# Seven experts' rows added to a DRAM buffer by an accumulating indirect DMA in place of the combine matmuls

## Chip, core and metric

The kernel runs on one core of a Trainium2 chip. The metric is the device time of one execution in microseconds (us), as a median of several runs.

## The reference

A decoder trunk of two layers for 256 tokens (SEQ) of width 1024 (D). Each layer mixes tokens by three branches (a state space model, dilated attention, attention into a memory), then applies a channel mixer: a dense SwiGLU in layer 0, and in layer 1 a mixture of eight experts of which each token uses two. Only the end of layer 1 is touched by the change:

```
logits = (t @ w_router)                       # t: 256 x 1024, 8 experts
top_v, top_i = lax.top_k(logits, 2)
wts = jax.nn.softmax(top_v, axis=-1)
gate = jnp.sum(jax.nn.one_hot(top_i, 8) * wts[..., None], axis=1)
for e in range(8):
    ye = swiglu(t, w_gate[e], w_up[e], w_down[e])   # 1024 -> 3584 -> 1024
    out = out + gate[:, e:e + 1] * ye
x = x + out
```

All of it is float32. An expert's weights are 44 MB, so that the eight experts read 352 MB from DRAM.

## The kernel before

The token rows lie in SBUF as x, 128 partitions by C = 2 chunks of 1024. All matmuls are done in three passes on a high and a low part of each operand (fp32r), so that float32 accuracy is kept. For the expert stage each weight matrix streams through a ring of RM = 7 tiles of 128 x 2048 floats (1 MB each; six in ring_e, the seventh in hT). An expert has 42 of them (MOE_TILES), 28 of gate and up weights and 14 of down weights. For each tile SyncE issues the load (L516) when VectorE has finished with the tile seven places ahead, ScalarE writes the high part into hi (L1788), VectorE the low part into lo (L2486), and TensorE does 12 matmuls of 512 columns with them (split_product, L736 to L738). hi and lo have three buffers each (H = 3), so that ScalarE starts on tile m when TensorE is done with tile m-3. SyncE, ScalarE, VectorE and TensorE each have their own program in a fixed order and are kept together by semaphores.

An expert works on the up to 128 tokens that chose it. DVE builds a 0/1 matrix `disp` (dispatch), 256 tokens by 128 slots, for two experts at a time; the matmuls of `gather` multiply it with the normed rows (h_hi, h_lo) and give `xe`, the transposed rows of the expert's slots, which are split into xe_hi and xe_lo. The order of the work on TensorE around the end of an expert is written out by hand:

- the last down tiles of expert e finish `y`, 128 slots by 1024, in PSUM banks 4 and 5
- gate_first(e + 1): the first two tiles of the next expert
- the *combine*: eight matmuls of 512 columns (L1344 and L1345) with dispT as the fixed operand and y_hi and y_lo as the moving one, which bring the rows of the slots back to the rows of the tokens in PSUM banks 3, 6, 7 and 2
- then expert(e + 1): its up tiles (2 and 3), two transposes of disp_plain (L1310), which VectorE copies to dispT (L2701), and the steps over the hidden columns.

ScalarE writes y_hi between the high parts of tiles 1 and 2 of the next expert (L1982), VectorE writes y_lo between the low parts (L2734). VectorE's add_rows (L2685) multiplies the four combined pieces with the token's gate and adds them to x, between tiles 3 and 4 of the next expert. After the last expert the adds go by halves and SyncE stores x into the output (L547). If more than 128 tokens chose one expert, a second pass follows; with these inputs none does.

GpSimd builds constants at the start and does small root calculations in the two mixers. In the expert stage it has no work. route_weights on VectorE (L2625 to L2631) computes the gates before the first expert.

Of the kernel before, what the change touches and what calls it, by code (L numbers as in the profile page):

```python
# [20 lines left out]
P = 128  # L21
# [11 lines left out]
def decoder_trunk(nc, x_in, mem_in, positions, norm_mix, w_in, a_re, a_im, log_dt, b_re, b_im,  # L33
# [57 lines left out]
    with ctx:  # L91
# [134 lines left out]
        fb("idle", [P, KD - 3, P])  # L226
        xe_hi = fb("xe_hi", [P, KD, P], F32R)
        xe_lo = fb("xe_lo", [P, KD, P], F32R)
        y_hi = fb("y_hi", [P, D], F32R)
# [15 lines left out]
        TURNS = MOE_TILES // RM  # L245

# [199 lines left out]
        def _(sp):  # L446
# [113 lines left out]
        def _(pool):  # L560
# [109 lines left out]
            for l in range(L):  # L670
# [36 lines left out]
                if l == 0:  # L707
# [4 lines left out]
                    rotary_gains(1)  # L712


        @block.tensor
        def _(pe):
# [490 lines left out]
            def experts():  # L1207
# [90 lines left out]
                def expert(pair, odd, last_one):  # L1298
# [9 lines left out]
                    pe.wait_ge(sem("added"), 4 * e + 1)  # L1308
                    for c in range(C):
                        last = nc.tensor.transpose(ps[:, 3, c * P:(c + 1) * P], disp_plain[:, c, odd, :], ident[:])  # L1310
                    last.then_inc(sem("dispatchT_done"), 1)
# [23 lines left out]
                    pe.wait_ge(sem("dispatchT_ready"), e + 1)  # L1335
                    for c, half in ADD_BY_HALVES if last_one else ADD_BY_ROWS:
                        if (c, half) == (0, 0) and last_one:
                            pe.wait_ge(sem("y_half_ready"), e // NE + 1)
                        elif c == 0 and half == (1 if last_one else 0):
                            pe.wait_ge(sem("y_ready"), e + 1)  # L1340
# [24 lines left out]
                def one_pass(pair0):  # L1365
# [6 lines left out]
                    if pair0 == 0:  # L1372
                        for p in range(NE // 2 - 1):
                            expert(p, 0, False)
                            expert(p, 1, False)
# [4 lines left out]
                    expert(NE // 2 - 1 + pair0, 0, False)  # L1380
# [5 lines left out]
                with pe.If(busiest > P):  # L1386
                    pe.wait_ge(sem("added"), 4 * NE + 1)
# [9 lines left out]
        def _(act):  # L1397
# [484 lines left out]
            def experts():  # L1882
# [53 lines left out]
                def expert(pair, odd, last_one):  # L1936
# [38 lines left out]
                    act.wait_ge(sem("added"), 4 * e + 1)  # L1975
                    rest = slice(0, D)
                    if last_one:
                        rest = slice(BANK, D)
                        act.wait_ge(sem("y_half_done"), e // NE + 1)
                        nc.scalar.activation(y_hi[:, 0:BANK], ps[:, 4, :], ACT.Copy).then_inc(sem("y_half_hi_ready"), 1)  # L1980
                    act.wait_ge(sem("split_used"), M + s0 + MOE_TILES)
                    nc.scalar.activation(y_hi[:, rest], flat_banks(4, 2)[:, rest], ACT.Copy).then_inc(  # L1982
                        sem("y_hi_ready"), 1)
# [3 lines left out]
                def one_pass(pair0):  # L1987
# [10 lines left out]
                    for p in range(NE // 2 - 1):  # L1998
                        expert(p + pair0, 0, False)
# [815 lines left out]
```

## Time and profile before

| | us |
|---|---|
| median of 3 runs | 1757.39 |
| lowest, highest | 1756.54, 1758.14 |
| the profiled execution, its time | 1759.97 |
| the profiled execution, span of the core | 1758.2 |
| mean granted clock of TensorE | 0.995 |

The profile is of one execution. Its times are us from the start of the span. PE is TensorE and PEld its weight loads, DVE is VectorE, ACT is ScalarE, POOL is GpSimd, SP is SyncE; a q behind a name is the engine's sequencer or DMA queue. L12 is line 12 of the kernel. In a row of the timeline stand the start, the duration, engine, line, operation, what is written `<-` what is read, the number of such instructions merged, and in brackets the idle time of the engine before it and what ended it. Matmuls are pipelined: the duration of one is longer than the time until the next starts. In a row of the waits stand who waited, for whom, us in total, how often, and the longest. The mixers and the dense layer take until about 765 us, the expert stage the rest.

### The profile page before, as it was taken

The numbers are of one execution on the slowest core, as the hardware profiler recorded it, in microseconds if no ns is written. First come the engines' busy times: TensorE is split into PE (matmuls) and PEld (weight loads), VectorE is DVE, ScalarE is ACT, GpSimd is POOL, SyncE is SP. The second block draws the span as 40 slices with busy tenths as digits, with TensorE's granted clock in tenths as the row PEclk, the third lists the DMA queues.
The fourth block names the chain that finished last, engine by engine and source line by source line (L and its number), as shares of the span: only waits on it lengthen the run. The fifth ranks groups of instructions, "written<-read, shape, count | busy, mean of one in ns | idle before, by whom it ended". The sixth has DMA issues, their size and how long they took to land.

```text
span 1758.2 us, 23343 instructions
## 1 busy us (share of the span) xinstructions
PE 1738.1 (99%) x8758; PEld 1439.0 (82%) x8758; DVE 1437.6 (82%) x1348; ACT 1191.4 (68%) x1405; POOL 119.6 (7%) x165
## 2 busy tenths in 40 slices
PE   9999999999999999999999999999999999999998
PEld 7778888888888888888888888888888888888886
DVE  8997557776649955768898898898998988988987
ACT  7877564744457756567777777767777767777775
POOL 5160000150002200000000000000000000000000
PEclk9999999999999999989999999999999999999999
DMA  7454336655444443479999999999999999999994
GB/s 242 141 167 142 123 122 214 209 185 180 167 162 152 154 151 120 159 265 369 377 351 338 381 362 367 375 343 360 364 354 374 357 350 379 349 373 374 364 370 166
DMA packets 221226, 477.09 MB, mean 271 GB/s; under 512 B 9357, under 2 KB 34057, under 8 KB 221129
## 3 DMA queue, kind: packets, MB, share of 16 engines
q1 hardware_dynamic: 220328, 474.07, 75.3%
q0 software_dynamic: 704, 1.70, 0.5%
q8 instruction: 62, 1.02, 0.2%
q14 instruction: 36, 0.29, 0.1%
q10 hardware_dynamic: 96, 0.02, 0.0%
HBM read 474.71 MB, written 1.05 MB: 271 GB/s over the span
## 4 chain that ended last, share of the span: by engine, by line
PE 88%; DVE 9%; issue 1%; ACT 1%; DMA 0%; SPq 0%; DVEq 0%; ACTq 0%
PE ps L736 27%; PE ps L738 26%; PE ps L737 26%; DVE ring_lo L2048 3%; PE ps L1271 1%; PE ps L1013 1%; PE ps L729 1%; DVE turned L2306 1%; PE ps L985 1%; DVE z L2264 1%; PE ps L1249 1%; PE ps L996 1%; ACT hi_m L1430 0%; DVE lo L2486 0%; PE ps L1345 0%
## 5 line engine op out<-in xcount | busy, mean ns | idle before, releaser
L2486 DVE TENSOR_TENSOR lo<-ring_e,hi 128x2048 fp32r<-128x2048 f32 x288 | 657.6, 2290 | 78.8 <-ACT hi L1788 76.9
L1788 ACT ACTIVATE hi<-ring_e 128x2048 fp32r<-128x2048 f32 x288 | 551.9, 1917 | 164.5 <-PE ps L738 164.5
L736 PE MATMUL ps<-hi,xe_hi 128*128 128x512 f32 x896 | 354.5, 396 | 1.7 <-DVE lo L2486 0.9
L738 PE MATMUL ps<-hi,xe_lo 128*128 128x512 f32 x896 | 349.6, 390 | 0.0
L737 PE MATMUL ps<-lo,xe_hi 128*128 128x512 f32 x896 | 349.0, 390 | 0.0
L1430 ACT ACTIVATE hi_m<-ring 128x1024 fp32r<-128x1024 f32 x160 | 160.6, 1054 | 115.9 <-PE ps L738 112.5
L2048 DVE TENSOR_TENSOR ring_lo<-ring,hi_m 128x1024 fp32r<-128x1024 f32 x160 | 190.2, 1231 | 33.6 <-ACT hi_m L1430 33.1
L738 PE MATMUL ps<-hi_m,xT_lo 128*128 128x512 f32 (+1 forms) x528 | 203.2, 385 | 0.0
L736 PEld LDWEIGHTS ps<-hi,xe_hi 128*128 128x128 f32 x896 | 168.3, 188 | 38.1 <-issue 3.7
L738 PEld LDWEIGHTS ps<-hi,xe_lo 128*128 128x128 f32 x896 | 168.2, 188 | 36.0
L737 PEld LDWEIGHTS ps<-lo,xe_hi 128*128 128x128 f32 x896 | 168.4, 188 | 33.2
L736 PE MATMUL ps<-hi,aT_hi 128*128 128x512 f32 x464 | 181.6, 391 | 0.1
L738 PE MATMUL ps<-hi,aT_lo 128*128 128x512 f32 x464 | 180.8, 390 | 0.0
L737 PE MATMUL ps<-lo,aT_hi 128*128 128x512 f32 x464 | 180.5, 389 | 0.0
L736 PE MATMUL ps<-hi_m,in_hi 128*128 128x512 f32 (+1 forms) x416 | 165.0, 397 | 5.1 <-DVE ring_lo L2048 3.8
L737 PE MATMUL ps<-ring_lo,in_hi 128*128 128x512 f32 (+1 forms) x416 | 159.6, 384 | 0.0
L2486 DVE TENSOR_TENSOR lo<-hT,hi 128x2048 fp32r<-128x2048 f32 x48 | 109.9, 2289 | 14.4 <-ACT hi L1788 14.1
L738 PEld LDWEIGHTS ps<-hi_m,xT_lo 128*128 128x128 f32 x528 | 99.7, 189 | 20.3
L1788 ACT ACTIVATE hi<-hT 128x2048 fp32r<-128x2048 f32 x48 | 92.0, 1916 | 20.8 <-PE ps L738 20.8
L736 PEld LDWEIGHTS ps<-hi,aT_hi 128*128 128x128 f32 x464 | 87.1, 188 | 18.3 <-issue 0.5
L738 PEld LDWEIGHTS ps<-hi,aT_lo 128*128 128x128 f32 x464 | 87.1, 188 | 18.3
L737 PEld LDWEIGHTS ps<-lo,aT_hi 128*128 128x128 f32 x464 | 87.2, 188 | 17.9
(422 smaller groups left out, 2464.5 us busy)
## 6 DMA issues: line engine op xcount, KB each, us to landing
ring_e<-in_moe_w_gate SPq DMA_DIRECT2D x104, 1024.0 KB, 6.9
ring_e<-in_moe_w_up SPq DMA_DIRECT2D x96, 1024.0 KB, 7.0
ring_e<-in_moe_w_down SPq DMA_DIRECT2D x88, 1024.0 KB, 6.7
ring<-in_w_in SPq DMA_DIRECT2D x50, 1024.0 KB, 5.0
hT<-in_moe_w_down SPq DMA_DIRECT2D x24, 1024.0 KB, 6.1
hT<-in_moe_w_up SPq DMA_DIRECT2D x16, 1024.0 KB, 6.4
ring<-in_ffn_w_gate SPq DMA_DIRECT2D x22, 512.0 KB, 3.9
ring<-in_ffn_w_up SPq DMA_DIRECT2D x22, 512.0 KB, 4.8
```

Of the source, the lines that this page charges most:

```text
L729: last = nc.tensor.transpose(o, a, ident[0:a.shape[0], 0:a.shape[0]])
L736: nc.tensor.matmul(o, x_hi, w_hi, start=first, stop=False, skip_group_check=True)
L737: nc.tensor.matmul(o, x_hi, w_lo, start=False, stop=False, skip_group_check=True)
L738: return nc.tensor.matmul(o, x_lo, w_hi, start=False, stop=end, skip_group_check=True)
L985: last = nc.tensor.matmul(ps[:, bank, col:col + nk], qkT[o:o + HD, 0, hd // 2, c * P:(c + 1) * P], qkT[o:o + HD, 1, hd // 2, 0:nk], start= ...
L996: nc.tensor.transpose(ps[:, 6 + b // 4, b % 4 * P:(b % 4 + 1) * P], pr[:, u % 2, b * P:(b + 1) * P], ident[:])
L1013: last = nc.tensor.matmul(ps[:, 5, o:o + v.shape[1]], pT[:, b * P:(b + 1) * P], v, start=first, stop=end, skip_group_check=True)
L1249: last = nc.tensor.matmul(o, part_[:, c, k * P:(k + 1) * P], disp[:, c].rearrange("p i s -> p (i s)"), start=i == 0 and c == 0, stop=i == ...
L1430: nc.scalar.activation(hi_m[:, m % 2, o], ring[:, n % R, o], ACT.Copy).then_inc(sem("mixer_hi_ready"), 1)
L1788: nc.scalar.activation(hi[:, m % H, :], src, ACT.Copy).then_inc(sem("hi_ready"), 1)
L2048: V.tensor_tensor(ring_lo[:, n % R, o], ring[:, n % R, o], hi_m[:, m % 2, o].bitcast(F32), ALU.subtract).then_inc(sem("mixer_lo_ready"), 1)
L2486: last = V.tensor_tensor(lo[:, m % H, :], src, hi[:, m % H, :].bitcast(F32), ALU.subtract)
```

## The change

Experts 0 to 6 are no longer combined by matmuls. A DRAM buffer `sums` of 384 rows is set to x (256 rows, and 128 spare rows). When an expert's `y` is finished, ScalarE writes it to SBUF as y_rows, multiplied with the gate of each slot's token, and GpSimd issues one indirect DMA that adds each of the 128 rows to the row of `sums` of its token; empty slots add to a spare row. At the end of the seven, GpSimd loads `sums` back into x, and the last expert (7) is combined and added as before.

Where the slot's token, whether it is filled, and its gate come from: a matrix `routes` (256 tokens by 8 experts by 4 values: the token's number, a one, and the high and low part of the gate) is multiplied with `disp` in two matmuls of 4 columns for each expert, in place of the two transposes of disp_plain. VectorE copies the result (128 x 4) to slot_values, and GpSimd computes with five small operations the row number and the gate of each slot.

The new small tiles take their room from the unused tile `idle`; each takes a multiple of 32 bytes, 480 in all, as `idle` loses, so that xe_hi, the gathered operand, stays at a multiple of 1024 bytes. y_rows lies at the place of y_hi. The second pass, if any, works as before.

```diff
-        fb("idle", [P, KD - 3, P])
+        routes = fb("routes", [P, C, NE, 4], F32R)
+        token_i = fb("token_i", [P, C], I32)
...
+        slot_gate = fb("slot_gate", [P, 1])
+        fb("idle", [P, (KD - 3) * P - 120])
...
+        y_rows = renamed("y_rows", [P, D], F32)
...
+        sums = nc.dram_tensor("sums", [SEQ + P, D], F32).ap()
@@ sync
-                sp.wait_ge(sem("added"), 4 * (NE - 1) + 3 + 2 * half)
+                sp.wait_ge(sem("added"), 3 + 2 * half)
@@ gpsimd
+            def expert_rows():
+                pool.wait_ge(sem("h_ready"), C)
+                pool.wait_ge(sem("h_hi_ready"), C)
+                chain(nc.gpsimd.iota(token_i[:], pattern=[[P, C]], base=0, channel_multiplier=1))
+                chain(nc.gpsimd.tensor_copy(token[:], token_i[:]))
+                nc.gpsimd.tensor_scalar(spare_row[:], token[:, 0:1], float(SEQ), None, ALU.add)
+                nc.gpsimd.tensor_copy(routes[:, :, :, 0], spread(token[:], 2, NE))
+                nc.gpsimd.tensor_copy(routes[:, :, :, 1], ones[:, 0:C * NE].rearrange("p (c e) -> p c e", c=C)).then_inc(
+                    sem("route_rows_ready"), 1)
+                pool.dma_start(sums[0:SEQ].rearrange("(c p) d -> p c d", p=P), x[:]).then_inc(sem("sums_set"), 16)
+                pool.dma_start(sums[SEQ:SEQ + P], x[:, 0, :]).then_inc(sem("sums_set"), 16)
+                for e in range(NE - 1):
+                    pool.wait_ge(sem("slot_values_taken"), e + 1)
+                    chain(nc.gpsimd.tensor_scalar(row_of[:], slot_values[:, 1:2], -1.0, 1.0, ALU.mult, ALU.add))
+                    chain(nc.gpsimd.tensor_tensor(row_of[:], row_of[:], spare_row[:], ALU.mult))
+                    chain(nc.gpsimd.tensor_tensor(row_of[:], row_of[:], slot_values[:, 0:1], ALU.add))
+                    if e > 0:
+                        pool.wait_ge(sem("rows_added"), 16 * e)
+                    chain(nc.gpsimd.tensor_copy(row_i[:], row_of[:]))
+                    nc.gpsimd.tensor_tensor(slot_gate[:], slot_values[:, 2:3], slot_values[:, 3:4], ALU.add).then_inc(
+                        sem("slots_ready"), 1)
+                    if e == 0:
+                        pool.wait_ge(sem("sums_set"), 16 * 2)
+                    pool.wait_ge(sem("rows_ready"), e + 1)
+                    pool.indirect_dma_start(sums, bass.IndirectOffsetOnAxis(row_i[:, 0:1], 0), y_rows[:], None,
+                                            compute_op=ALU.add).then_inc(sem("rows_added"), 16)
+                pool.wait_ge(sem("rows_added"), 16 * (NE - 1))
+                pool.dma_start(x[:], sums[0:SEQ].rearrange("(c p) d -> p c d", p=P)).then_inc(sem("x_summed"), 16)
@@ tensor: expert, scattered is True for experts 0 to 6
+                    if scattered:
+                        pe.wait_ge(sem("added"), 1)
+                        pe.wait_ge(sem("routes_ready"), 1)
+                        pe.wait_ge(sem("route_rows_ready"), 1)
+                        if e > 0:
+                            pe.wait_ge(sem("slot_values_taken"), e)
+                        for c in range(C):
+                            last = nc.tensor.matmul(ps[:, 3, 0:4], disp[:, c, odd, :], routes[:, c, e, :], start=c == 0,
+                                                    stop=c == C - 1)
+                        last.then_inc(sem("slot_values_done"), 1)
...
                     if not last_one:
                         gate_first(e + 1)
-                    pe.wait_ge(sem("dispatchT_ready"), e + 1)
+                    if scattered:
+                        pe.wait_ge(sem("rows_ready"), e + 1)
+                        return
@@ scalar: expert
+                    if scattered:
+                        act.wait_ge(sem("slots_ready"), e + 1)
+                        if e > 0:
+                            act.wait_ge(sem("rows_added"), 16 * e)
+                        act.wait_ge(sem("split_used"), M + s0 + MOE_TILES)
+                        nc.scalar.activation(y_rows[:], flat_banks(4, 2), ACT.Copy, scale=slot_gate[:]).then_inc(
+                            sem("rows_ready"), 1)
@@ vector: route_weights
+                chain(V.tensor_copy(routes[:, :, :, 2], gate[:]))
+                V.tensor_tensor(routes[:, :, :, 3], gate[:], routes[:, :, :, 2].bitcast(F32), ALU.subtract).then_inc(
+                    sem("routes_ready"), 1)
@@ vector: expert, no add_rows and no y_lo where scattered
+                    if scattered:
+                        dve.wait_ge(sem("slot_values_done"), e + 1)
+                        if not first_one:
+                            dve.wait_ge(sem("slots_ready"), e)
+                        V.tensor_copy(slot_values[:], ps[:, 3, 0:4]).then_inc(sem("slot_values_taken"), 1)
...
                     if last_one:
+                        if first_pass:
+                            dve.wait_ge(sem("x_summed"), 16)
                         add_rows(e_here, e, ADD_BY_HALVES)
```

## Rows read from the trace of the kernel before

**Rows 1.** The page's busy times: us, share of the span, instructions.
```profile
PE 1738.1 (99%) x8758; PEld 1439.0 (82%) x8758; DVE 1437.6 (82%) x1348; ACT 1191.4 (68%) x1405; POOL 119.6 (7%) x165
```
**Rows 2.** The waits of all engines from 850 to 1740 us.
```profile
ACT hi L1788 <- PE ps L738: 168.5, 197, 2.2
...
PEld ps L736 <- issue: 3.5, 7, 0.5
```
**Rows 3.** The waits of SyncE's own DMA queue in the same stretch.
```profile
SPq L516 <- DVE lo L2486: 698.8, 303, 4.2
```
**Rows 4.** Timeline of TensorE around the combine of expert 2.
```profile
1147.27 0.39 PE L1344 MATMUL ps<-y_hi,dispT 128*128 128x512 f32 x1
...
1149.08 0.39 PE L736 MATMUL ps<-hi,xe_hi 128*128 128x512 f32 x1
...
1154.52 0.38 PE L1310 MATMUL ps<-ident,disp_plain 128*128 128x128 f32 x2
1154.66 0.47 PE L736 MATMUL ps<-hi,xe_hi 128*128 128x512 f32 x1
```
**Rows 5.** Instructions on disp_plain: ns min/median/max, first and last start us.
```profile
L1310 PE MATMUL ps<-ident,disp_plain x16: 270/270/271, 790.5 to 1642.5; 128*128 128x128 f32 x16
```
**Rows 6.** Stretch of seven experts: PE, PEld, DVE, ACT, POOL busy; clock; DMA share; GB/s.
```profile
790.50:1642.50 852.00, 851.25 (x3892) 704.14 (x3891) 770.29 (x467) 622.23 (x413) 0.00 (x0) 1.00 0.99 363
```
**Rows 7.** Timeline of TensorE: small matmuls and the gather matmuls.
```profile
770.47 0.35 PE L1233 MATMUL ps<-sel,before_r 128*128 128x8 f32 x1
770.68 0.35 PE L1234 MATMUL ps<-sel,ones_r 128*128 128x8 f32 x1
...
1160.90 0.40 PE L1249 MATMUL ps<-disp,h_lo 128*128 128x256 f32 x2
1161.14 0.40 PE L1249 MATMUL ps<-disp,h_hi 128*128 128x256 f32 x2
```
**Rows 8.** Timeline of VectorE between experts 2 and 3.
```profile
1143.71 1.22 DVE L2734 TENSOR_TENSOR y_lo<-ps,y_hi 128x1024 fp32r<-128x1024 f32 x1
...
1149.25 2.72 DVE L2685 SCALAR_TENSOR_TENSOR x<-ps,gate,x 128x512 f32<-128x512 f32 x4
```
**Rows 9.** Timeline of ScalarE between the same experts.
```profile
1141.73 1.03 ACT L1982 ACTIVATE y_hi<-ps 128x1024 fp32r<-128x1024 f32 x1 [0.80 <-PE ps L738]
1142.65 1.91 ACT L1788 ACTIVATE hi<-ring_e 128x2048 fp32r<-128x2048 f32 x1
...
1147.96 1.91 ACT L1788 ACTIVATE hi<-ring_e 128x2048 fp32r<-128x2048 f32 x1
```
**Rows 10.** Timeline of VectorE and TensorE before the first expert.
```profile
785.11 0.17 DVE L2631 TENSOR_TENSOR gate<-gate,rstat 128x16 f32<-128x16 f32 x1
785.32 2.29 DVE L2486 TENSOR_TENSOR lo<-ring_e,hi 128x2048 fp32r<-128x2048 f32 x1
...
787.67 0.50 PE L736 MATMUL ps<-hi,xe_hi 128*128 128x512 f32 x1 [0.94 <-DVE lo L2486]
```
**Rows 11.** Timeline of VectorE and GpSimd in the dense layer.
```profile
378.31 0.42 DVE L2168 TENSOR_TENSOR b_tmp_next<-b_raw_next,spT 128x256 f32<-128x256 f32 x1
...
380.00 2.13 DVE L2168 TENSOR_TENSOR b_tmp_next<-b_raw_next,spT 128x256 f32<-128x256 f32 x1
...
379.76 2.08 POOL L625 TENSOR_TENSOR cT<-cT,spT 128x1024 f32<-128x1024 f32 x1 [4.96 <-ACT cT L1854]
```
**Rows 12.** Timeline: issue of expert 3's first tile, and its first reader.
```profile
1120.71 3.09 SPq L516 DMA_DIRECT2D ring_e<-in_moe_w_gate  x2
...
1136.80 1.91 ACT L1788 ACTIVATE hi<-ring_e 128x2048 fp32r<-128x2048 f32 x1
```
**Rows 13.** Loads into ring_e from 850 to 1740 us, issue to landing.
```profile
DMA to landing us min/median/max: 4.8/6.8/8.2
```
**Rows 14.** DMA in 744 to 764 us, GB/s in 40 slices.
```profile
GB/s 0 41 16 303 389 397 406 430 163 234 315 422 393 328 385 406 410 401 418 406 414 393 418 406 418 397 406 418 414 401 402 418 414 406 401 418 397 422 397 418
```
**Rows 15.** The page's DMA issues: KB each, median us from issue to landing.
```profile
out<-x SPq DMA_DIRECT2D x2, 512.0 KB, 3.7
```

More of the change, by code:

```diff
@@ L1296, in gate_first, with expert @@
                     hidden(0, FFN_TILES, MOE_TILES * e, e)
-                def expert(pair, odd, last_one):
+                def expert(pair, odd, last_one, scattered=False):
                     e = 2 * pair + odd
@@ L1306, in expert @@
                     hidden(1, M + 2, s0)
[L1308 to L1311, printed above, removed]
+                    if scattered:
[8 more added lines that the diff above has]
+                        last.then_inc(sem("slot_values_done"), 1)
+                    else:
+                        ci = combines_before(e)
+                        pe.wait_ge(sem("added"), 4 * ci + 1)
+                        pe.wait_ge(sem("slot_values_taken"), NE - 1)
+                        for c in range(C):
+                            last = nc.tensor.transpose(ps[:, 3, c * P:(c + 1) * P], disp_plain[:, c, odd, :], ident[:])
+                        last.then_inc(sem("dispatchT_done"), 1)
                     def step(f, shift, first, between=None, gathers=None):
@@ L1386, in experts @@
                 with pe.If(busiest > P):
-                    pe.wait_ge(sem("added"), 4 * NE + 1)
+                    pe.wait_ge(sem("added"), 4 * combines_before(NE) + 1)
                     one_pass(NE // 2)
@@ L1934, in gathered_high, with expert @@
                         sem("xe_hi_ready"), 1)
-                def expert(pair, odd, last_one):
+                def expert(pair, odd, last_one, scattered=False):
                     e = 2 * pair + odd
@@ L1973, in expert @@
                             split(i, e + 1)
[L1975 to L1983, printed above, removed]
+                    if scattered:
[5 more added lines that the diff above has]
+                            sem("rows_ready"), 1)
+                    else:
+                        act.wait_ge(sem("added"), 4 * combines_before(e) + 1)
+                        act.wait_ge(sem("rows_added"), 16 * (NE - 1))
+                        rest = slice(0, D)
+                        if last_one:
+                            rest = slice(BANK, D)
+                            act.wait_ge(sem("y_half_done"), e // NE + 1)
+                            nc.scalar.activation(y_hi[:, 0:BANK], ps[:, 4, :], ACT.Copy).then_inc(
+                                sem("y_half_hi_ready"), 1)
+                        act.wait_ge(sem("split_used"), M + s0 + MOE_TILES)
+                        nc.scalar.activation(y_hi[:, rest], flat_banks(4, 2)[:, rest], ACT.Copy).then_inc(
+                            sem("y_hi_ready"), 1)
                     if not last_one:
@@ L1998, in one_pass @@
                     for p in range(NE // 2 - 1):
-                        expert(p + pair0, 0, False)
-                        expert(p + pair0, 1, False)
-                    expert(NE // 2 - 1 + pair0, 0, False)
+                        expert(p + pair0, 0, False, not base)
+                        expert(p + pair0, 1, False, not base)
+                    expert(NE // 2 - 1 + pair0, 0, False, not base)
                     expert(NE // 2 - 1 + pair0, 1, True)
@@ L2687, in add_rows, with expert @@
                                                ALU.add).then_inc(sem("added"), 1)
-                def expert(e_here, pair, odd, first_one, last_one):
+                def expert(e_here, pair, odd, first_one, last_one, scattered=False):
                     e = 2 * pair + odd
+                    ci = combines_before(e)
+                    first_pass = scattered or last_one and isinstance(e, int) and e < NE
                     a0 = NF + NFE * e
@@ L2694, in expert @@
                     split(3, e)
-                    if not first_one:
+                    if not first_one and not first_pass:
                         add_rows(e_here - 1, e - 1)
@@ L2725, in expert @@
                             split(i, e + 1)
+                    if scattered:
+                        split(2, e + 1)
+                        return
                     rest = slice(0, D)
```

39 lines of the change are left out of this document (25 added, 14 removed).

## The prediction

> **What bounds the kernel now.** I read the page's busy times first, and only as a question: TensorE is busy for 99% of the span [rows 1], but ends of matmuls are modelled, and the weights stream from DRAM all the while, so it could as well be the DMA. The waits of the expert stage (850 to 1740 us) answer it. ScalarE waits for TensorE to hand back a half buffer, 168.5 us in total; TensorE's only entry is 3.5 us in seven pieces of 0.5 us [rows 2]. The queue of SyncE, which issues the weight loads, sat for 698.8 of 890 us until VectorE had finished with a ring buffer [rows 3]: the loads are not late, they wait for room. So TensorE sets the pace. The timeline says how fast: eight combine matmuls start at 1147.27 and the next weight matmul at 1149.08, so 0.226 us for each 512-column matmul, whatever their 0.39 us of pipelined duration. One expert has 42 tiles of 12 such matmuls, 504 x 0.226 = 114 us; the transposes of disp_plain, two an expert, give its period, (1642.5 - 790.5)/7 = 121.7 us [rows 5]. The other 7 are the combine 1.8, transposes, gathers and a stall of half a us. In those 852.0 us TensorE is busy for 851.3 [rows 6]. There is no slack on TensorE: an instruction taken out there is time.
>
> **What is removed.** For experts 0 to 6, TensorE loses the eight combine matmuls: 8 x 0.226 = 1.81 us each, 7 x 1.81 = **12.7 us**. They lie bare on the path, between two weight matmuls, with no wait before or after [rows 4]. ScalarE's y_hi becomes y_rows, the same size from the same banks in the same place (1.03 us; with a scale from a tile I allow 0.1 more) and gains nothing. VectorE loses y_lo (1.22 us) and four adds into x (2.72 us) [rows 8]. Those are off the path (VectorE is idle a tenth of the stage [rows 6]), so I count them zero; they buy slack.
>
> **What is swapped.** Two transposes of disp_plain (next instruction 0.14 us after the first: 1154.52 to 1154.66 [rows 4]) become two matmuls of four columns with disp as operand. No such matmul is in the trace. Below: as cheap as the transposes, 0.14 the pair. Above: the eight-column matmuls at 770.47, 0.21 each, 0.42 the pair, though right behind a wait of TensorE. Nearest are the gather matmuls, each with one 128x128 weight load as well, 0.12 each (two pairs 0.24 apart) [rows 7]: 0.24. So +0.1 each, 7 x 0.1 = **0.7 us** lost (bounds 0 and 2.0).
>
> **What is added on VectorE at the start.** Two small operations behind L2631 split the gates, at a spacing of 785.11 to 785.32, 0.21 each. Here VectorE *is* the path: they stand in front of the split of tile 3, and TensorE idled 0.94 us at 787.67 for exactly that [rows 10]. **0.4 us** lost (bounds 0 and 0.4).
>
> **GpSimd and the new DMAs.** GpSimd does nothing in the expert stage now [rows 6]. Five small operations an expert, an indirect DMA of 128 rows of 4 KB, and at the ends 1.5 MB stored to sums and 1 MB read back. The store starts when h_lo is done, before the first expert, the read-back right behind the scatter of expert 6, 115 us before the last expert's adds ask for it (wait for x_summed). Each scatter likewise has a whole expert until rows_added is asked for. As latency all is hidden, even at many times the 3.7 us of the 0.5 MB store of the output [rows 15]. If the cover were gone, each us would count once. What can hurt is sharing. An expert's weights are 42 tiles of 1024 KB, 44.04 MB in 121.7 us, 362 GB/s; in the first fill, with the queue full, the later slices show 393 to 422 [rows 14]. After the change the need is 367 plus the scatter: 0.52 MB plainly moved is 1.3 us at 410, with the destination read as well 2.6 us. Tile 0 of the next expert was issued at 1120.71 and first read at 1136.80, 16.1 us later [rows 12]; landing takes 6.8 us, 8.2 at worst [rows 13]. So 7.9 us of slack against 1.3 to 2.6 us of push, and room of 40 GB/s to recover it before the next. Cost zero.
>
> **New waits.** TensorE waits for rows_ready where it waited for dispatchT_ready and y_ready: after gate_first of the next expert. y_rows is done when y_hi was, 1141.73 + 1.03 = 1142.76 [rows 9], and TensorE comes at 1147.27: no stall. But it now runs on to tile 2 at 1147.27 instead of 1149.08. Is tile 2 split? ScalarE's half ends at 1142.65 + 1.91 = 1144.56 [rows 9], VectorE's takes 2.29 more [rows 10], 1146.9: 0.4 us to spare, 0.3 with a longer y_rows. Tile 4: ScalarE ends 1147.96 + 1.91 = 1149.87, VectorE 1152.2; TensorE comes at 1147.27 + 5.44 (24 matmuls, 1149.08 to 1154.52 [rows 4]) + 0.24 = 1152.95: 0.8 to spare. This margin is thin, so I bound it: 0, which I take, to 0.5 us an expert, 3.5 in all, the size of the stalls already there. Those seven (start of tile 0, 0.5 us against a regular 0.23) stay; were they to go, 7 x 0.27 = 1.9 gained. x_summed, routes_ready and route_rows_ready are ready long before they are asked for, if GpSimd's first five operations fit between the second h_lo and 790.5, where L1310 stands now [rows 5]. The new `idle` with the new small tiles is to leave xe_hi where it stood; I count no effect.
>
> **Sum.** 12.7 - 0.7 - 0.4 = 11.6 us gained; bounds 12.7 - 2.0 - 0.4 - 3.5 = 6.8 and 12.7 + 1.9 = 14.6. The profiled execution took 1759.97 us (span 1758.20 and 1.77 around it), 2.6 over the median 1757.39. So 1748.4 for one like it, and a median of 1757.4 - 11.6 = **1745.8 us**, own range 1742.8 to 1750.6.
>
> **Rivals.** (A) *The scatter holds the weight loads; slower.* If an accumulate must read a row, add and write it before its engine takes another packet, 8 rows an engine go one after the other. The 0.5 MB store lands in 3.7 us [rows 15], of which 1.3 are bytes at 410 GB/s, so 2.4 are the way there and back; 8 x 2.4 = 19 us, less 7.9 of slack, 11 us of stall x 7 = 78, time 1757.4 + 78 - 11.6 = 1824. It decides from 7.9 + 11.6/7 = 9.6 us of delay a scatter. For: nothing in the trace shows that it doesn't, none of its DMAs accumulates. Against: each tile lands in 6.8 us while a new one is asked for every 2.9 (121.7/42), so the engines hold packets of two or three transfers at once already.
>
> (B) *DMA is the true pace.* If 362 GB/s is what the chip gives this stream, removing matmuls only exposes loads, and each scatter adds 1.05 MB, 2.9 us: 7 x 2.9 and the 2.6 MB of store and read-back 7.2 more, 27.5 in all, near 1785. Against: SyncE waits for room, not for bytes [rows 3], and the 393 to 422 of the first fill [rows 14]. "DMA: Bandwidth & Descriptors" in the Trainium skill (section Bandwidth) puts the HBM side at about 358 GB/s a core and says that it binds for DRAM to SBUF. By that figure an expert's weights would need 123 us and the change would gain nothing. The trace disagrees with it here, where one core runs alone: 393 and more.
>
> (C) *GpSimd and VectorE get in each other's way; a part of the gain goes.* At 380.00 a VectorE operation that took 0.42 us at 378.31 took 2.13, beside a GpSimd one that began at 379.76 and took 2.08 [rows 11]. GpSimd's operations are some 0.2 us here, and the margins above are 0.3 to 0.8 us. At 0.5 to 1 us an expert, 3.5 to 7 us lost: 1749 to 1753. "SBUF — State Buffer" in the Trainium skill (section SBUF: two separate sides) calls the pair of ports an exclusive lock for a whole instruction, and names VectorE operations with two SBUF inputs, which each split is. By that rule, with which the trace agrees [rows 11], VectorE loses up to 5 x 0.2 us an expert. VectorE is idle for 852.0 - 770.3 us in seven experts, 11.7 each [rows 6], so it should not show on TensorE, unless it falls where margins are thin.
>
> (D) *Nothing measurable*: stalls of 1.2 to 2.2 us an expert eat the gain, 1754 to 1761.
>
> **Chances.** Forecast (1742 to 1750) 0.60, C 0.14, D 0.08, A 0.09, B 0.05, more gain than its bound 0.04. Faster by over 0.2% (3.5 us, about what a measurement of this kernel can tell) is forecast, C and more: 0.78; same 0.08; slower 0.14. The range 1742 to 1757 holds the forecast, C and most of D: 0.60 + 0.14 + 0.06.
>
> **What would show it.** The experts repeat every 120.0 us instead of 121.7; no L1344/L1345 kind of matmul before the last expert; the wait for rows_ready shows no entry; VectorE's busy time falls by 7 x (1.22 + 2.72) = 28 us. Wrong if TensorE's waits name a DMA or `lo` with more than 1 us an expert, if landings of weight tiles beside a scatter go over 15 us (A) or are longer everywhere with SyncE no longer waiting (B), or if splits last 2.5 us and more beside GpSimd's operations (C).

## The result, and the profile after

The changed kernel takes **1745.62 us** (median of 6 runs, 1743.96 to 1746.58) and the kernel before 1757.41 (6 runs on the same chip): a ratio of 0.9932, 95% interval 0.9919 to 0.9945, 11.8 us less. The prediction said 1745.8. The profiled execution took 1744.81 us (span 1742.7, clock 0.998).

The busy times of the page, against [rows 1], and two of its DMA queues:

```profile
PE 1722.3 (99%) x8702; PEld 1425.7 (82%) x8702; DVE 1411.3 (81%) x1315; ACT 1192.3 (68%) x1405; POOL 174.9 (10%) x215
...
q1 hardware_dynamic: 220328, 474.07, 75.4%
q0 software_dynamic: 2400, 8.00, 1.9%
```

TensorE has 56 instructions fewer, seven times eight. VectorE lost 26.3 us. The queue of GpSimd's DMAs (q0) is where the scatters are.

The waits from 850 to 1740 us, against [rows 2] (who waits, for whom, us in total, times, longest):

```profile
POOL sums L753 <- ACT y_rows L2042: 717.1, 7, 104.3
ACT hi L1850 <- PE ps L784: 154.8, 195, 1.8
...
POOL x L756 <- DMA sums<-y_rows,row_i: 9.0, 1, 9.0
...
PEld ps L782 <- issue: 3.5, 7, 0.5
```

Up to the combine of the last expert TensorE still waits for nothing but the seven times 0.5 us; neither a DMA nor `lo` is among what stops it. GpSimd waits 717 of 890 us for the next y_rows, so its program is never late, except by 9.0 us at the read-back, which nobody waits for.

The timeline of TensorE where the combine of expert 2 was, against [rows 4]:

```profile
1145.98 0.39 PE L784 MATMUL ps<-hi,xe_lo 128*128 128x512 f32 x1
1146.20 0.28 PE L1361 MATMUL ps<-routes,disp 128*128 128x4 f32 x2
1146.34 0.48 PE L782 MATMUL ps<-hi,xe_hi 128*128 128x512 f32 x1
1146.66 0.40 PE L783 MATMUL ps<-lo,xe_hi 128*128 128x512 f32 x1
```

The next weight matmul starts 0.14 us after the two slot matmuls (L1361), as it did after the two transposes. But 0.14 us isn't all that a pair takes: the matmul after that one starts 0.32 us later, where 0.23 is regular. From the last weight matmul ahead of the pair to the second behind it (1145.98 to 1146.66) it is 0.68 us, and two spacings without a pair are 0.45. So the pair takes 0.23 us. The kernel before shows the same for the transposes, 0.68 us from 1154.29 to 1154.97:

```profile
1154.29 0.39 PE L738 MATMUL ps<-hi,xe_lo 128*128 128x512 f32 x1
...
1154.97 0.39 PE L737 MATMUL ps<-lo,xe_hi 128*128 128x512 f32 x1
```

VectorE, ScalarE and GpSimd in the same place, against [rows 8, 9]:

```profile
1138.17 4.49 DVE L2558 TENSOR_TENSOR lo<-ring_e,hi 128x2048 fp32r<-128x2048 f32 x2 [0.91 <-ACT hi L1850]
1143.38 4.61 DVE L2558 TENSOR_TENSOR lo<-ring_e,hi 128x2048 fp32r<-128x2048 f32 x2 [0.71 <-ACT hi L1850]
...
1135.22 1.12 ACT L2042 ACTIVATE y_rows<-ps,slot_gate 128x1024 f32<-128x1024 f32 x1 [0.82 <-PE ps L784]
...
1136.62 2.13 POOL L753 DMA_INDIRECT sums<-y_rows,row_i  x1 [100.89 <-ACT y_rows L2042]
1148.74 0.19 POOL L742 TENSOR_SCALAR row_of<-slot_values 128x1 f32<-128x1 f32 x1 [10.00 <-DVE slot_values L2782]
1149.03 0.26 POOL L743 TENSOR_TENSOR row_of<-row_of,spare_row 128x1 f32<-128x1 f32 x1
1149.37 4.52 POOL L744 TENSOR_TENSOR row_of<-row_of,slot_values 128x1 f32<-128x1 f32 x1
```

The scatter goes out at 1136.62, as soon as y_rows is written. One of GpSimd's small operations lasted 4.52 us where 0.19 is usual: it began at 1149.37, just after VectorE began the first of two splits at 1149.35 (they end at 1151.63 and 1153.84), and it ended at 1153.89, with the second. The same operation lasted 4.52 us in three of the seven experts. Its result is wanted some 100 us later.

The stretch of seven experts, against [rows 6] (us, then busy us of PE, PEld, DVE, ACT, POOL, granted clock, DMA share, GB/s):

```profile
787.56:1626.92 839.36, 838.57 (x3835) 693.73 (x3834) 743.87 (x432) 623.00 (x413) 50.44 (x42) 1.00 1.01 371
```

An expert takes 839.36/7 = 119.91 us in place of 121.71. That is 1.80 less each and 12.6 in all (852.0 - 839.4). From the first expert matmul to the slot matmuls of expert 0 it is 12.69 us against 12.33: 0.36 lost. So the change is worth 12.6 - 0.36 = 12.2 us by the trace. The two spans differ by 15.5; the other 3.3 us lie ahead of the expert stage, in code that the change doesn't touch. They are most likely a difference of the two executions, as the 2.6 us of the profiled execution before over its median are; no run was made to separate them.

The DMAs from 850 to 1730 us: the two queues (packets, MB, share of 16 engines), issues with the us to landing, and loads into ring_e from 850 to 1740 us, against [rows 13]:

```profile
q1 hardware_dynamic: 133753, 318.23, 96.6%
q0 software_dynamic: 1280, 4.72, 2.4%
...
x<-sums POOLq DMA_DIRECT2D x1, 1024.0 KB, 8.6
sums<-y_rows,row_i POOLq DMA_INDIRECT x7, 10.9
```
```profile
DMA to landing us min/median/max: 4.8/7.2/12.2
```

From these comes the price of a scatter. The weights take 0.966 x 880 / 318.23 = 2.67 us of all 16 engines for a MB. q0 takes 0.024 x 880 = 21.1 us for seven scatters (3.67 MB) and the read-back (1.05 MB, at 2.67 2.8 us). That leaves 18.3/7 = **2.6 us a scatter**, 5.0 us a MB, nearly twice what plain bytes cost. This is an estimate from the time that the packets took (the share is given to a tenth of a per cent, so 2.5 to 2.7). The worst landing of a weight tile went from 8.2 to 12.2 us. From the landing of a tile to ScalarE's first read of it there were at least 7.1 us in experts 1 to 7 before (worked out tile by tile from the trace); in experts 1 to 6 there are now at least 5.5, and 3.2 in the last one, beside the read-back.

### The profile page after: what moved, and what is told of

It is laid out like the page before. It is cut to its first block, busy times and chain, and to the rows that moved or that the text cites. A ratio compares the mean times of both kernels' runs of the same rounds, so it can differ in the third digit from the quotient of the medians.

```text
span 1742.7 us, 23237 instructions
## 1 busy us (share of the span) xinstructions
PE 1722.3 (99%) x8702; PEld 1425.7 (82%) x8702; DVE 1411.3 (81%) x1315; ACT 1192.3 (68%) x1405; POOL 174.9 (10%) x215
## 4 chain that ended last, share of the span: by engine, by line
PE 87%; DVE 9%; issue 1%; ACT 1%; DMA 0%; DVEq 0%; ACTq 0%
PE ps L782 27%; PE ps L784 27%; PE ps L783 26%; DVE ring_lo L2120 3%; PE ps L1317 1%; PE ps L1059 1%; PE ps L775 1%; DVE turned L2378 1%; PE ps L1031 1%; DVE z L2336 1%; PE ps L1295 1%; PE ps L1042 1%; ACT hi_m L1492 0%; DVE lo L2558 0%; DVE costab L2255 0%
## 5 line engine op out<-in xcount | busy, mean ns | idle before, releaser
L1850 ACT ACTIVATE hi<-hT 128x2048 fp32r<-128x2048 f32 x48 | 92.0, 1916 | 21.1 <-PE ps L784 21.1
L784 PEld LDWEIGHTS ps<-hi,aT_lo 128*128 128x128 f32 x464 | 87.1, 188 | 18.3
L782 PEld LDWEIGHTS ps<-hi,aT_hi 128*128 128x128 f32 x464 | 87.1, 188 | 18.2 <-issue 0.4
```

Of the source, the lines that this page charges most:

```text
L782: nc.tensor.matmul(o, x_hi, w_hi, start=first, stop=False, skip_group_check=True)
L784: return nc.tensor.matmul(o, x_lo, w_hi, start=False, stop=end, skip_group_check=True)
L1850: nc.scalar.activation(hi[:, m % H, :], src, ACT.Copy).then_inc(sem("hi_ready"), 1)
```

## The experiments

Each changes the changed kernel. Ratios are to the kernel before on the same chip; the changed kernel's own is 0.9932.

**1. TensorE's time alone back.** Eight matmuls of 512 columns, with operands that lie ready, into the banks of the old combine, unused.

```diff
                     if scattered:
                         pe.wait_ge(sem("rows_ready"), e + 1)
+                        for c, half in ADD_BY_ROWS:
+                            o = ps[:, ADD_BANKS[2 * c + half], :]
+                            d = slice(half * BANK, (half + 1) * BANK)
+                            nc.tensor.matmul(o, before_r[:], h_hi[:, c, d], start=True, stop=False)
+                            nc.tensor.matmul(o, before_r[:], h_hi[:, c, d], start=False, stop=True)
                         return
```

> The kernel after the change, with eight matmuls of 512 columns (before_r as the fixed operand, the normed rows as the moving one, into the same four banks, results unused) put back on TensorE at the place of the combine, for experts 0 to 6. Theory 1 (the gain is TensorE time): 8 x 0.226 us x 7 = 12.7 us slower than the changed kernel, so about 1758, the time before; an expert every 121.7 us again. Theory 2 (the gain came from VectorE, which lost y_lo and four adds an expert and now splits tiles earlier): no more than 2 us slower than the changed kernel, 1746 to 1748.

Measured: 1757.06 us (10 runs; before 1756.83 in 25), ratio 1.0002 [0.9992, 1.0011]. The slot matmuls come every 121.71 us again, as in [rows 5]. With these matmuls back the whole gain is gone, although the scatter stays and VectorE stays relieved. So all of the gain is TensorE's time.

**2. VectorE's work alone back.** The four adds (into an unused place) and the subtraction for y_lo, at their old places in VectorE's program.

```diff
+                    elif not first_one:
+                        aside = memT[:].rearrange("p k t -> p (k t)")
+                        for i, (c, half) in enumerate(ADD_BY_ROWS):
+                            o = slice(half * BANK, (half + 1) * BANK)
+                            V.scalar_tensor_tensor(aside[:, i * BANK:(i + 1) * BANK], ps[:, 4 + half, :],
+                                                   gate[:, c, bass.ds(e_here, 1)], h_lo[:, c, o].bitcast(F32),
+                                                   ALU.mult, ALU.add)
...
+                        dve.wait_ge(sem("rows_ready"), e + 1)
+                        V.tensor_tensor(y_lo[:], ps[:, 4:6, :].rearrange("p b n -> p (b n)"), y_rows[:], ALU.subtract)
```

> The kernel after the change, with VectorE's removed work put back in its places: a subtract of 128x1024 from PSUM before the split of tile 2, and four multiply-adds of 128x512 between the splits of tiles 3 and 4 (results unused), 3.9 us an expert. Theory 1 (TensorE alone sets the pace): same as the changed kernel, 1745.6 within 2 us, but the margin of tile 4 is thin: without the combine TensorE comes 1.8 us earlier than it did, and tile 4's low part ends 3.9 us later than now, near the moment at which TensorE asks; a stall of up to 1 us an expert, 7 in all, is possible. Theory 2 (VectorE's relief is the gain): back at 1757.

Measured: 1755.09 us (10 runs), ratio 0.9988 [0.9979, 0.9998]: 9.8 us of the gain are lost (0.0056 x 1757). Timelines of TensorE and VectorE in it, between experts 2 and 3:

```profile
1149.75 0.28 PE L1361 MATMUL ps<-routes,disp 128*128 128x4 f32 x2
1151.24 0.47 PE L782 MATMUL ps<-hi,xe_hi 128*128 128x512 f32 x1 [1.21 <-DVE lo L2558]
```
```profile
1141.78 4.49 DVE L2558 TENSOR_TENSOR lo<-ring_e,hi 128x2048 fp32r<-128x2048 f32 x2
1146.18 2.72 DVE L2779 SCALAR_TENSOR_TENSOR memT<-ps,gate,h_lo 128x512 f32<-128x512 f32 x4
1148.82 4.48 DVE L2558 TENSOR_TENSOR lo<-ring_e,hi 128x2048 fp32r<-128x2048 f32 x2
```

The adds end at 1148.9, the low part of tile 4 at 1151.1. TensorE, which now skips the combine, would start on it at 1149.89 (1149.75 + 0.14) and waits 1.35 us more, seven times: 9.4 us. In the kernel before, TensorE spent 1.8 us on the combine meanwhile.

**3. No scatter.** The indirect DMAs and the waits for them are out, so that the rows of experts 0 to 6 don't reach the output; all else stays.

```diff
-                    pool.indirect_dma_start(sums, bass.IndirectOffsetOnAxis(row_i[:, 0:1], 0), y_rows[:], None,
-                                            compute_op=ALU.add).then_inc(sem("rows_added"), 16)
```

> The kernel after the change without the seven indirect DMAs and the waits on them; the rows of experts 0 to 6 are left out of the result. Theory 1 (the scatter is hidden): the same time, 1745.6 within 2 us, and the least time between landing and first reading of a weight tile back at 7 us from 5.5. Theory A (the scatter holds the weight loads enough to be seen): faster by more than 3.5 us.

Measured: 1744.14 us (4 runs), ratio 0.9932 [0.9915, 0.9948]. The scatter costs nothing that can be measured. The least slack of a weight tile, from its landing to ScalarE's first read, is 6.7 us in experts 1 to 6, near the 7.1 of before.

**4 to 6. Two, four and eight scatters.** The same rows are also added to one, three or seven other DRAM buffers, and all must have landed where one had to.

```diff
+                    for other in others:
+                        pool.indirect_dma_start(other, bass.IndirectOffsetOnAxis(row_i[:, 0:1], 0), y_rows[:], None,
+                                                compute_op=ALU.add).then_inc(sem("rows_added"), 16)
```

> As the changed kernel with two indirect DMAs an expert. Theory 1: 5.2 us of engine time an expert against 7 us of slack: no cost, 1745.6 within 2 us, the least slack of tiles 1 to 41 about 4 us. If a scatter's cost were proportional from the first one on: a quarter of what four cost, 2 to 3 us slower.

> The kernel after the change with four indirect accumulating DMAs an expert in place of one; the three more add the same rows to three other DRAM buffers that nothing reads. One scatter took 1.5 us off the slack of the weight tiles. Theory 1 (a scatter costs its engines' time alone, some 2.6 us, and its packets mix with the loads): four take 10.4 us of engine time an expert; the loads need 44.04 MB at 400 to 410 GB/s, 107 to 110 of 119.9 us, so that it just fits or misses by 1 us an expert, and the least slack falls to 0 to 2 us: 0 to 10 us slower than the changed kernel, 1746 to 1756. Theory A (rows go one after the other and hold an engine for 2.4 us each): 77 us of blocked engines an expert, over 1900 us. Theory B (the DMA was at its limit already): 7 x 7.8 = 55 us slower, 1800.

> As the run with four indirect DMAs an expert, now with eight (seven more buffers that nothing reads). Four cost about 9 us in all, with the slack of the weight tiles used up for tiles 9 to 13 of each expert. Theory 1 (only the engines' time counts, 2.6 us a scatter, against 7 us of slack at first and 10 to 12 us of free engine time an expert): 20.9 us an expert, 9 to 14 us more than is free, 7 times: 65 to 95 us slower than the changed kernel, 1810 to 1840. Theory A' (rows of scatters block each other or the loads beyond their own time, in one scatter too little to be seen): more than 150 us slower.

| scatters an expert | us (runs) | ratio, interval | over the changed kernel, us |
|---|---|---|---|
| 2 | 1745.16 (4) | 0.9932 [0.9915, 0.9948] | 0 |
| 4 | 1754.11 (10) | 0.9982 [0.9972, 0.9992] | 8.8 |
| 8 | 1826.62 (2) | 1.0395 [1.0375, 1.0416] | 81 |

The last column is the difference of the ratios times 1757. Waits from 850 to 1740 us with four, then with eight:

```profile
ACT hi L1854 <- DMA ring_e<-in_moe_w_gate: 17.8, 13, 3.1
```
```profile
ACT hi L1854 <- DMA ring_e<-in_moe_w_gate: 90.4, 15, 10.3
...
PE ps L786 <- DVE lo L2562: 58.6, 15, 9.0
```

Now ScalarE waits for weight tiles, then VectorE for it and TensorE for VectorE: rival A's chain. Seven more scatters of 2.6 us are 18.2 us of engine time against the 5.5 us of slack that one leaves, 12.7 late, 7 x 12.7 = 89 us; 81 were measured. Three more are 7.8 against 5.5, 16 us by the same reckoning; 8.8 were measured. The reckoning is rough, and that it comes near 81 is in part chance. By the trace TensorE, from the slot matmuls of expert 0 to the end, is idle for 58 us more than in the changed kernel, 8.3 an expert and not 12.7. The other 21 us are longer running: in each expert TensorE stands still for 5.7 to 9.0 us at once, and the granted clock falls within that stop to 0.50 (1.2 GHz) for 6.8 to 10.2 us. One such piece, with clock 0.50, in the run with eight:

```profile
1058.90:1069.10 10.20, 5.34 (x12) 3.84 (x12) 4.06 (x2) 4.92 (x3) 0.38 (x2) 0.50 1.05 353
```

With four scatters the clock stays at 1.00 in the seven experts. The least slack is 2.1 us with two in experts 1 to 6 and 0.02 with four: it ends between them. The first scatter took 1.6 us of it (7.1 to 5.5), the second 3.4, so it doesn't shrink evenly.

**7. The operands moved by 32 bytes.** The filler tile ahead of xe_hi is eight values a partition longer, so that xe_hi, xe_lo and what lies behind them move by 32 bytes. Nothing else changes.

```diff
-        fb("idle", [P, (KD - 3) * P - 120])
+        fb("idle", [P, (KD - 3) * P - 112])
```

> The changed kernel with 32 bytes more of the unused tile idle, so that xe_hi, xe_lo, y_hi and all behind them lie 32 bytes further on and the gathered operand is no longer at a multiple of 1024 bytes. Theory 1 (the place of xe_hi does not matter): the same time, the matmuls of 512 columns still 0.2265 us apart. Theory P (a weight load reads an operand more slowly off a multiple of 1024 bytes): weight loads over 188 ns or matmuls further apart; with 1 ns more on each of 2688 matmuls with xe 2.7 us slower, with 10 ns 27 us.

Measured: **1759.97 us** (10 runs), ratio 1.0016 [1.0006, 1.0026]: 14.8 us above the changed kernel, more than the change gains. TensorE's groups from 790 to 1640 us (instructions, busy us, mean ns of one, idle), changed kernel first, then the moved one:

```profile
L782 PE MATMUL ps<-hi,xe_hi 128*128 128x512 f32 x797 | 315.2, 395 | 0.8
...
L782 PE MATMUL ps<-hi,aT_hi 128*128 128x512 f32 x339 | 132.6, 391 | 0.0
```
```profile
L782 PE MATMUL ps<-hi,xe_hi 128*128 128x512 f32 x781 | 312.8, 401 | 0.9
...
L782 PE MATMUL ps<-hi,aT_hi 128*128 128x512 f32 x336 | 131.5, 391 | 0.0
```

Each matmul on xe takes 5 or 6 ns more; those on aT, which didn't move, take what they took. xe is the fixed operand here, the one that is loaded as weights; the moving operands hi and lo lie ahead of the filler and didn't move. The weight loads themselves last 188 ns on the mean in both kernels. The stretch of seven experts is 852.63 us for 839.36. Its 2352 matmuls on xe (28 tiles x 12 x 7) make that 5.6 ns each, and 2688 in eight experts 15.2 us.

**8, 9. Moved by 1024 and by 512 bytes.** The filler is 256, then 128 values longer.

> The filler tile ahead of the gathered operand is 256 values a partition longer, so that the operand and what lies behind it move by 1024 bytes and the operand stays at a multiple of 1024. Theory (it is the place within 1024 bytes that counts): the expert matmuls stay at 226 to 227 ns, 1745 to 1746 us, ratio 0.9932. Rival (it is the place relative to another buffer, or the one address, that counts): 232 to 235 ns and about 1760 us, ratio 1.0016, as with 32 bytes.

> The filler tile is 128 values a partition longer: the operand lies 512 bytes past a multiple of 1024. Theory (a multiple of 1024 is wanted, since a matmul reads 512 bytes a partition of it at a time, k by k, in pairs of 1024): slower, somewhere up to the 14.5 us of the shift by 32 bytes, 1750 to 1760 us. Rival (it is enough that each 512-byte slice starts on a boundary of its own size, or of 64 bytes or more): as the changed kernel, 1745 to 1746 us, ratio 0.9932.

Measured: 1745.76 us, ratio 0.9932 [0.9915, 0.9948], and 1745.17 us, ratio 0.9933 [0.9916, 0.9950] (4 runs each; before 1757.57). The group with 512 bytes:

```profile
L782 PE MATMUL ps<-hi,xe_hi 128*128 128x512 f32 x797 | 315.4, 396 | 0.8
```

Both are as fast as the changed kernel. So not the one address counts, nor a multiple of 1024: 512 is enough, 32 is not. What lies between wasn't tried. No run moved xe alone; but it is the only operand of the slower matmuls that moved.

**10. GpSimd kept busy.** Four additions of 128 x 1024 on GpSimd behind each scatter, into an unused place.

```diff
+                    spare = memT[:].rearrange("p k t -> p (k t)")
+                    for _ in range(4):
+                        chain(nc.gpsimd.tensor_tensor(spare[:, 0:D], spare[:, D:2 * D], spare[:, D:2 * D], ALU.add))
```

> The changed kernel with four GpSimd adds of 128x1024 from and to SBUF behind each scatter (results unused), at the place with the thin margins of tiles 2 and 4. Such an operation took 2.08 us before. Theory C (a GpSimd operation that reads SBUF and a VectorE split keep each other out for the whole of an operation): VectorE starts its splits up to 2.1 us later, four times, with about 3 us of idle time and 0.8 us of margin there: 3 to 5 us of stall an expert, 20 to 35 us slower than the changed kernel, with splits of 4 us and more in the trace. Theory 1 without C: no change.

Measured: 1783.93 us (4 runs), ratio 1.0151 [1.0134, 1.0168], 38 us above the changed kernel. GpSimd and VectorE at the same boundary:

```profile
1149.57 14.19 POOL L757 TENSOR_TENSOR memT<-memT 128x1024 f32<-128x1024 f32 x4
```
```profile
1149.54 16.36 DVE L2561 TENSOR_TENSOR lo<-ring_e,hi 128x2048 fp32r<-128x2048 f32 x4 [0.91 <-ACT hi L1853]
```

Four splits, 9.0 us by themselves (two take 4.49), last 16.36: the two engines take turns, each starts one in the midst of the other's and is held until that one ends. The splits of all experts, of this kernel and then of the changed one (duration ns min/median/max, first and last start us):

```profile
L2561 DVE TENSOR_TENSOR lo<-ring_e,hi x275: 2275/2293/4823, 786.9 to 1738.4; 128x2048 fp32r<-128x2048 f32 x138
```
```profile
L2558 DVE TENSOR_TENSOR lo<-ring_e,hi x283: 2278/2292/2318, 786.7 to 1724.9; 128x2048 fp32r<-128x2048 f32 x142
```

And by its waits TensorE stands for `lo`:

```profile
PE ps L785 <- DVE lo L2561: 28.1, 25, 2.2
```

So C's mechanism is real. 7 us more of VectorE at each boundary cost 5.5 on TensorE. By the trace 28 of the 38 us are idle time of TensorE and the rest is longer running; behind such stops the granted clock stood at 0.50 (1.2 GHz) for three pieces of 3.4 us in the seven experts. GpSimd's own small operations in the change hold no split up: the longest of them is 2318 ns against a median of 2292.

**11, 12. VectorE's order at the boundary, and at the start.** What remains is 7 x 0.27 us at tile 0 and 1.67 us before the fourth tile at the start. The first run splits each half tile right after the low part of that half of xe; the second also moves the choice of the first experts' tokens, the count of the busiest expert and the route table (three groups of VectorE's operations) behind later splits, and with them the slot matmuls of expert 0.

```diff
-                        for i in range(2):
-                            split(i, e + 1)
+                            split(half, e + 1)
```
```diff
+                            if f == 1 and i == 2 and first_one and scattered:
+                                for half in range(2):
+                                    first_odd(half)
+                        if f == 1 and first_one and scattered:
+                            busiest_expert()
+                            route_weights()
...
-                        for half in range(2):
-                            first_odd(half)
-                        busiest_expert()
-                        route_weights()
```

> Only VectorE's order at the change of expert differs: the low part of one half of the gathered columns is followed at once by the split of that half, where the changed kernel takes both low parts and then both splits. Theory (VectorE's queue sets when TensorE gets the first low part of the next expert): the 0.27 us that TensorE waits there in each of seven experts goes, 1.9 us in all, about 1743.7 us on the chip of the changed kernel's runs, a ratio to before near 0.992. Rival (the wait moves to the second half, since the sum of VectorE's work before it is the same): the same time as the changed kernel, 0.9932.

> The order of the run before, and at the start of the expert stage the choice of the first expert's tokens, the count and the route table are moved behind splits that TensorE waits for, with expert 0's slot matmuls after its third step. Theory: of the 1.67 us that TensorE waits there before the fourth tile, up to 1.4 us goes as well, in all 3.3 us less than the changed kernel, about 1742.3 us, ratio 0.9913. Rival (the wait there is for the gathered operand and not for VectorE's queue): no more than the run before, 0.992 or 0.9932.

Measured: 1745.17 us, ratio 0.9932 [0.9916, 0.9949], and 1743.59 us, ratio 0.9928 [0.9912, 0.9945] (4 runs each). The stretch of seven experts in the first, and in the second TensorE's two stops in expert 0:

```profile
788.59:1627.45 838.86, 838.37 (x3835) 694.05 (x3834) 744.34 (x432) 622.15 (x413) 50.70 (x42) 1.00 1.01 371
```
```profile
785.63 0.47 PE L782 MATMUL ps<-hi,xe_hi 128*128 128x512 f32 x1
```
```profile
798.25 0.47 PE L782 MATMUL ps<-hi,aT_hi 128*128 128x512 f32 x1 [0.95 <-DVE lo L2565]
```

0.5 us are gained in seven experts and not 1.9: most of the stop went from tile 0 to tile 2 (there now 0.46 us between two matmuls in place of 0.23). At the start the stop at the fourth tile, 1.67 us from one matmul to the next, is down to 0.37, and one of 1.34 us (by the same spacing) stands in its place 13 us later. From the first expert matmul to the last expert's transposes it is 852.05 us in the changed kernel, 851.56 and 851.50 in these two. So neither is a measurable gain over the changed kernel. In the first run the rival held as it was written: the wait moved, since VectorE's sum of work is the same. In the second only the rival's time held, not its reason. It said that TensorE waits there for the gathered operand; but the stop at the fourth tile went from 1.67 to 0.37 us when VectorE's queue ahead of it got shorter, so it was VectorE's queue, and the wait came back later as the work did.

## Why the prediction was right

**The pace.** It took TensorE for the bound and 0.226 us for what a matmul costs. Run 1 shows it by itself: 56 matmuls back, whole gain gone. The seven combines gave 12.6 us by the trace; the terms 12.7 - 0.7 said 12.0.

**The swap, off by its whole size.** The slot matmuls were put at 0.24 a pair from the gather matmuls, 0.7 us lost; they lose nothing, and the lower bound was right. What was wrong is the price of what they replace. The prediction read 0.14 us for the two transposes from the first spacing behind them, and 0.24 for the gather matmuls from the steady spacing of a row of pairs. Counted to the second matmul behind them, the transposes took 0.23 and the slot matmuls take 0.23, so 0.24 was a good price for the new pair and the 0.1 of difference was none.

**The start.** 0.4 us predicted, 0.36 found: the stop that was 0.94 in [rows 10] is 1.28.

```profile
784.66 0.50 PE L782 MATMUL ps<-hi,xe_hi 128*128 128x512 f32 x1 [1.28 <-DVE lo L2558]
```

**How near, and why.** The terms gave 11.6 us, the medians differ by 11.8 and the trace gives 12.2. That it came within 0.2 us is in part luck: the swap was 0.7 us too dear, and the medians show 0.4 us less than the trace. Runs of the changed kernel are up to 2.6 us apart.

**New waits.** Zero, as taken, and the margins came out nearly as worked out. By the prediction VectorE is done with tile 2 0.4 us before TensorE wants it, with tile 4 0.8 us before. In the profile these are 1140.4 (half of the pair from 1138.17) against 1140.74, and 1145.7 against 1146.34: 0.3 and 0.6. The seven half-microsecond stops stayed, as taken.

**VectorE's relief: right that it gives nothing, wrong in weight.** The prediction counted y_lo and the adds zero and said that they "buy slack". Against the kernel before that holds: without their 26 us the kernel with its matmuls back is no faster (run 1). But of the 11.8 us, 9.8 hang on them (run 2). The arithmetic was at hand: with the adds of [rows 8] in place VectorE is free at 1149.25 + 2.72 = 1151.97 and done with tile 4 at 1154.26, against TensorE's 1152.95, 1.3 us late; 1.35 were measured. A change that had taken out the matmuls alone would have shown rival D's time, 1755.1 in its 1754 to 1761.

**The scatter.** Taken as hidden, 1.3 to 2.6 us of push against 7.9 of slack. By packet time it is the upper figure, 2.6; the least slack of a tile was 7.1 and not 7.9, it shrank to 5.5, and TensorE felt nothing. Rival A's point of decision was 9.6 us of delay a scatter; four scatters, some 10.4 us of engine time, cost 8.8 us of the gain's 12, eight cost 81. So scatters can hold the loads, and one is a quarter of what it takes. Its 19 us for a scatter, rows one after the other with 2.4 us each, was wrong: it lands in 10.9 us in the midst of the loads. Rival B is out: the loads now run at 371 GB/s without a wait of TensorE. The 358 GB/s that "DMA: Bandwidth & Descriptors" of the Trainium skill (section Bandwidth) gives for the HBM side would have allowed no gain, and this is above it for 839 us on end. The same section says that its own single-core measurements, up to 425 GB/s, were made with the pair's other core idle, and that each core gets about 358 when both stream. The prediction left that out; one core runs here, and 371 agrees with it.

**GpSimd beside VectorE.** Small operations of GpSimd were held up to 4.5 us by splits, no split by a small operation. With long operations it costs 38 us (run 10). "SBUF — State Buffer" in the Trainium skill (section SBUF: two separate sides) tells of a lock that the operation which starts first holds for its whole length while the other is blocked; in run 10 the trace agrees, where long operations of the two engines alternate. The 4.52 us of a small operation go beyond it: it began inside one split and ended only with the next. Why it was held for two isn't shown.

**The place of xe_hi.** "I count no effect" held only since the diff shortens `idle` by just what the new tiles take. One that had let them slip by 32 bytes would have come out at 1760 us, slower than before, by a term that the prediction had not priced (run 7). No other term of this size stood in the prediction with neither bound nor chance.

## What to carry to other kernels

Where one engine is never idle, its instructions are time at their spacing; the rest of a change decides only whether the gain can be kept, so work out for each other engine when it is done and when it is now wanted, with and without the work that the change takes from it. Put a number on the slack of the streams before a new DMA is added: here one accumulating scatter used 1.6 of 7.1 us, and four were too many. When the cost of a short instruction is read from a timeline, count to where the regular spacing is back, and not to the next start. When small tiles are added to SBUF, look where the large operands end up, and compare the mean of one matmul before and after.

## What the hardware showed that was not expected

- A move by 32 bytes of the tiles from xe_hi on, the fixed operands of the matmuls among them, took a 512-column fp32r matmul on xe_hi from a mean of 395 to 401 ns and cost 14.8 us in 2688 matmuls; moves by 512 and 1024 bytes cost nothing.
- Accumulating rows cost the DMA engines some 5.0 us a MB by packet time where weight loads cost 2.67, and 128 rows of 4 KB land 10.9 us after the issue in the midst of 371 GB/s of loads. GpSimd is occupied with the issue for up to 2.15 us.
- GpSimd's operations on 128 x 1 values, 0.19 us each, last up to 4.52 us when they meet splits of VectorE, two splits long, and the splits stay at 2.29; four long ones stretch four splits from 9.0 to 16.4 us.
- A pair of matmuls of four columns with a new fixed operand each takes 0.23 us of TensorE's time, as much as a pair of transposes of 128 columns and about as much as a pair of gather matmuls of 256 (0.24).
- Stops of TensorE of 5.7 to 9.0 us cost more than themselves: the granted clock fell to 0.50 for 6.8 to 10.2 us at each (run with eight scatters).
